# Expert weights in halves: every 2 MB load of an MoE stage split into two 1 MB transfers with semaphores of their own

## What is computed

```python
def hier_moe(n, w_rg, w_re, w_gate, w_up, w_down):
    ...
    hg = jnp.einsum("nd,edf->nef", t, w_gate)
    hu = jnp.einsum("nd,edf->nef", t, w_up)
    act = jax.nn.silu(hg) * hu * gates[..., None].astype(t.dtype)
    return jnp.einsum("nef,efd->nd", act, w_down).reshape(bt, s, d)
```

## Time and profile before

| | |
|---|---|
| median of three runs | 1160.43 us |
| the profiled execution's own time | 1159.52 us |
| its span, first to last instruction | 1157.7 us |
| mean granted TensorE clock | 0.981 of full speed |
| PE busy | 1059.5 us (92%), 7153 matmul instructions |
| DVE, ACT, POOL busy | 550.9, 200.3, 42.4 us |
| DMA | 384.53 MB in 38612 packets, mean 332 GB/s |
| gate and up loads | 64 transfers of 2048 KB, median 27.8 us from issue to landing |
| down loads | 32 transfers of 2048 KB, median 26.1 us from issue to landing |

### The profile page before, as it was taken

The page is one execution under the profiler, slowest core; times in us unless marked ns, Lnnn a source line. Parts: engine busy times, 40 slices in busy tenths (PEclk is TensorE's granted clock), DMA queues, the critical chain, the costliest instruction groups (busy, mean ns, idle before and its releaser), DMA issues.

```text
span 1157.7 us, 17262 instructions
## 1 busy us (share of the span) xinstructions
PE 1059.5 (92%) x7153; PEld 588.5 (51%) x7153; DVE 550.9 (48%) x1078; ACT 200.3 (17%) x457; POOL 42.4 (4%) x38
## 2 busy tenths in 40 slices
PE   8998999998999999999999998899998969797885
PEld 3576776666666656677777542333332323232221
DVE  3583565356535466474434116545443434343333
ACT  1111012131213231311011021111211111111020
POOL 0030110001020000010000000000000000000000
PEclk9899999999999999999999999999999999999898
DMA  9989337988999989743776538999999999999994
GB/s 326 360 233 354 119 133 304 354 336 318 373 380 395 396 331 374 301 166 109 280 286 232 204 132 357 428 412 429 427 425 430 425 428 431 427 427 428 427 428 163
DMA packets 38612, 384.53 MB, mean 332 GB/s; under 512 B 4863, under 2 KB 7551, under 8 KB 10207
## 3 DMA queue, kind: packets, MB, share of 16 engines
q1 hardware_dynamic: 35968, 375.83, 81.1%
q0 software_dynamic: 1568, 5.62, 1.8%
q10 hardware_dynamic: 1008, 2.10, 0.5%
HBM read 375.63 MB, written 7.90 MB: 331 GB/s over the span
## 4 chain that ended last, share of the span: by engine, by line
PE 70%; DMA 16%; DVE 8%; issue 2%; ACT 2%; POOL 1%; ACTq 0%; DVEq 0%; SPq 0%; POOLq 0%
PE ps L605 22%; DMA arena<-w_gu 10%; PE ps L597 7%; PE ps L1025 6%; PE ps L1002 5%; PE ps L1056 5%; DMA arena<-w_proj 4%; PE ps L1040 4%; PE ps L799 4%; PE ps L766 3%; PE ps L587 3%; DMA arena<-w_dn 2%; DVE cst L1775 1%; PE ps L1061 1%; DVE cst L1714 1%
## 5 line engine op out<-in xcount | busy, mean ns | idle before, releaser
L605 PE MATMUL ps<-arena 128*128 128x256 f32 x1456 | 337.2, 386 | 7.9 <-DMA arena<-w_proj 4.5
L605 PEld LDWEIGHTS ps<-arena 128*128 128x128 f32 x1456 | 273.5, 192 | 60.3 <-issue 13.9
L1025 PE MATMUL ps<-arena,cst 128*32 128x512 f32 x1024 | 122.2, 613 | 29.7 <-DMA arena<-w_gu 28.0
L1775 DVE STREAM_TRANSPOSE cst<-ps 128x512 f32<-128x512 f32 x31 | 22.2, 717 | 172.5 <-PE ps L1002 172.5
L597 PE MATMUL ps<-arena 128*64 128x256 f32 x832 | 101.3, 385 | 0.0
L1002 PE MATMUL ps<-arena,cst 128*32 128x512 f32 (+1 forms) x768 | 95.6, 612 | 0.0
L1040 PE MATMUL ps<-arena,stat 128*32 128x512 f32 x512 | 68.0, 652 | 24.6 <-DVE stat L1779 23.2
L1025 PEld LDWEIGHTS ps<-arena,cst 128*32 128x32 f32 x1024 | 32.4, 112 | 113.7 <-issue 82.6
L597 PEld LDWEIGHTS ps<-arena 128*64 128x64 f32 x832 | 55.1, 136 | 37.8 <-issue 14.1
L1797 DVE COPY arena<-ps 32x512 f32<-32x512 f32 x64 | 44.2, 691 | 48.0 <-PE ps L1040 46.6
L1056 PE MATMUL ps<-arena,cst 128*128 128x512 f32 x128 | 57.0, 598 | 9.6 <-ACT cst L1267 9.6
(11 more groups left out here) (261 smaller groups left out, 980.9 us busy)
## 6 DMA issues: line engine op xcount, KB each, us to landing
arena<-w_gu SPq DMA_DIRECT2D x64, 2048.0 KB, 27.8
arena<-w_dn SPq DMA_DIRECT2D x32, 2048.0 KB, 26.1
arena<-w_proj SPq DMA_DIRECT2D x43, 1024.0 KB, 8.1
arena<-kc SPq DMA_DIRECT2D x16, 2048.0 KB, 9.8
arena<-vc SPq DMA_DIRECT2D x16, 2048.0 KB, 8.9
arena<-w_o SPq DMA_DIRECT2D x16, 1024.0 KB, 4.9
arena<-kc SPq DMA_DIRECT2D x8, 1024.0 KB, 8.8
arena<-vc SPq DMA_DIRECT2D x8, 1024.0 KB, 10.1
```

The costliest lines, as they stand in the source:

```text
L605: last = mm(psum[:, regions(v)[j - 1]], left[a], right[:, a], start=first and opens and a == 0, stop=final and a == 1, skip_group_check=True)
L1025: last = mm(ps[g:g + 32, 0, :], xgT[:, s % 2, kt, :], w[:, k, :], start=kt < 4, stop=kt >= KT - 4)
```

## The change

Each piece is loaded as two transfers of 1 MB, and everything that hangs on a piece hangs on its half. A gate and up piece is cut after four of its eight blocks, a down piece after the first of its two blocks; each partition then gets 8 KB per transfer. Every slot has two load semaphores. PE waits for a half before the first matmul that reads it and counts it as used behind the last one; `piece_used` counts halves, six for an expert. SP waits for each half's area by itself. The matmuls, their order and their operands stay as they were, and the waits of ACT and DVE are renumbered.

```diff
-        ring_loaded = [sem(f"ring_loaded{k}") for k in range(RING)]
+        ring_loaded = [[sem(f"ring_loaded{j}_{k}") for k in range(2)] for j in range(RING)]
...
+            def half_piece(u, e, k):
+
+                loaded = (once_loaded[u] if u in once else ring_loaded[slot(u)])[k]
+                if u % 3 < 2:
+                    h = KT // 2 * (u % 3) + 4 * k
+                    sp.dma_start(gate_up(u)[:, 4 * k:4 * k + 4], w_gu[e, :, h:h + 4]).then_inc(loaded, 16)
+                else:
+                    sp.dma_start(down(u)[:, k], w_dn[e, :, k]).then_inc(loaded, 16)
+
             def piece(u, e):
...
+                for k in range(2):
+                    half_piece(u, e, k)
...
             for u in range(10, 3 * BODY + 10):
-                sp.wait_ge(piece_used, u - 9 if u < 16 else u - 7)
-                piece(u, u // 3)
+                for k in range(2):
+                    sp.wait_ge(piece_used, 2 * (u - 10 if u < 16 else u - 8) + k + 1)
+                    half_piece(u, u // 3, k)
...
-                    sp.wait_ge(piece_used, i * (3 * BODY) + (j + 3))
...
+                    for k in range(2):
+                        sp.wait_ge(piece_used, i * (6 * BODY) + (2 * j + k + 5))
...
-                        loaded(i, first, 3 * s + h)
                         w = gate_up(3 * s + h if first else 3 * s + h + 3 * BODY)
                         for k in range(KT // 2):
                             kt = KT // 2 * h + k
                             g = 32 * (kt % 4)
+                            if k % 4 == 0:
+                                loaded(i, first, 3 * s + h, k // 4)
                             last = mm(ps[g:g + 32, 0, :], xgT[:, s % 2, kt, :], w[:, k, :],
                                       start=kt < 4, stop=kt >= KT - 4)
-                        last.then_inc(piece_used, 1)
+                            if k % 4 == 3:
+                                last.then_inc(piece_used, 1)
...
-                    loaded(i, first, 3 * s + 2)
                     w = down(3 * s + 2 if first else 3 * s + 2 + 3 * BODY)
                     pe.wait_ge(ye_copied, i * (4 * BODY) + 4 * (s + 1))
                     for j in range(2):
+                        loaded(i, first, 3 * s + 2, j)
                         for g in range(4):
                             last = mm(ps[32 * g:32 * g + 32, 3, :], actT[:, j, :], w[:, j, 512 * g:512 * g + 512],
                                       start=j == 0, stop=j == 1)
-                    last.then_inc(piece_used, 1)
+                        last.then_inc(piece_used, 1)
```

More of the change, by code:

```diff
@@ L225, in hybrid_step @@
         once = {6: A_N2, 7: A_N2 + PIECE}
-        once_loaded = {u: sem(f"once_loaded{u}") for u in once}
+        once_loaded = {u: [sem(f"once_loaded{u}_{k}") for k in range(2)] for u in once}
         def slot(u):
@@ L519, in _ @@
             sp.dma_start(mst, mst_d).then_inc(mst_loaded, 16)
-            def piece(u, e):
[L522 to L527, removed]
+            def half_piece(u, e, k):
[5 more added lines that the diff above has]
+                    sp.dma_start(down(u)[:, k], w_dn[e, :, k]).then_inc(loaded, 16)
+            def piece(u, e):
+                for k in range(2):
+                    half_piece(u, e, k)
             for o in range(1, 13):
@@ L555, in pieces @@
                         e = sp.value_load(eblk_i[0:1, ds(i * BODY + u // 3, 1)], min_val=0, max_val=NEXP - 1)
-                    sp.wait_ge(piece_used, i * (3 * BODY) + (j + 3))
[L557 to L561, removed]
+                    for k in range(2):
+                        sp.wait_ge(piece_used, i * (6 * BODY) + (2 * j + k + 5))
+                        if u % 3 < 2:
+                            h = KT // 2 * (u % 3) + 4 * k
+                            sp.dma_start(area(A_R[slot(u)], KT // 2, 2 * FF)[:, 4 * k:4 * k + 4], w_gu[ds(e, 1), :, h:h + 4]).then_inc(ring_loaded[slot(u)][k], 16)
+                        else:
+                            sp.dma_start(down(u)[:, k], w_dn[ds(e, 1), :, k]).then_inc(ring_loaded[slot(u)][k], 16)
             sp.wait_ge(blocks_ready, 1)
@@ L1004, in gather, with loaded @@
                 last.then_inc(xg_mm, 1)
-            def loaded(i, first, u):
+            def loaded(i, first, u, k):
                 if first and u in once:
-                    pe.wait_ge(once_loaded[u], 16)
+                    pe.wait_ge(once_loaded[u][k], 16)
                 elif first and u < 6:
-                    pe.wait_ge(ring_loaded[u], 16)
+                    pe.wait_ge(ring_loaded[u][k], 16)
                 else:
-                    pe.wait_ge(ring_loaded[(u - 2) % RING], i * 48 + 16 * ((u - 2) // RING + 1))
+                    pe.wait_ge(ring_loaded[(u - 2) % RING][k], i * 48 + 16 * ((u - 2) // RING + 1))
             def experts(i, first, final):
@@ L1255, in experts @@
                     b = s % BATCH
-                    act.wait_ge(piece_used, i * (3 * BODY) + (3 * s + 2))
+                    act.wait_ge(piece_used, i * (6 * BODY) + (6 * s + 4))
                     copy(part, ps[:, 0, :]).then_inc(gu_copied, 1)
@@ L1259, in experts @@
                     nc.scalar.activation(sg, ps[:, 2, 0:64], ACT.Silu).then_inc(silu_done, 1)
-                    act.wait_ge(piece_used, i * (3 * BODY) + (3 * s + 3))
+                    act.wait_ge(piece_used, i * (6 * BODY) + (6 * s + 6))
                     if first and s == 0:
@@ L1794, in experts @@
                         scale_rows(0, P).then_inc(p_made, 1)
-                    dve.wait_ge(piece_used, i * (3 * BODY) + (3 * s + 3))
+                    dve.wait_ge(piece_used, i * (6 * BODY) + (6 * s + 6))
                     for g in range(2, 4):
```

## The result

The changed kernel takes 1166.72 us (median of 22 runs, 1161.63 to 1168.21), the kernel before in the same series 1164.05 us (22 runs, 1158.29 to 1169.84). The ratio is **1.0027, with a 95% interval of 1.0014 to 1.0040**: 0.27% or about 3 us slower. Against the kernel beside it the forecast was 1.7 us slower (0.15%), at the low edge of that interval; the measured change lies inside the 0.3% called "no change". The forecast in microseconds missed: 1166.72 is 4.6 us above the 1162.1 forecast and just above the range's end of 1166.5. Of these 4.6 us, 3.6 are the level, for the kernel before was itself that much slower over 22 runs than over the three that the forecast was hung on, and the rest is the change.

What follows compares the result with a forecast made beforehand. The DMA engines were taken to bound the experts' stage; start -0.9, rate +4.6 and tail -2.0 us on 1159.5 gave 1161.2, or 1162.1 us on the median, range 1156.9 to 1166.5.

Steps and rivals of the forecast that it cites:

- the 0.3% called "no change": Whole kernel: about 3.5 us is what a measurement can tell from no change; chance of a result within it 0.58.
- The bound: Experts' stage, about 700 us to the end: lasts as long as DMA engines need for pieces 10 to 95, about 421 us.
- The rate, +4.6 us: DMA engines, 86 pieces: nine more packets per engine and piece at 6 ns cost 4.6 us, ends 0 and +8.9.
- the rival that the prediction gave 0.20: Every DMA engine, all 86 pieces: packet price 8 to 11.5 ns, sum +3.3 to +6.0 us; chance 0.20.
- The two prices that the 6 ns were put between: Packet prices from the two longest saturated stretches with mostly 8 KB rows, taken as nearest in size.
- The 2.0 us per transfer: DMA stream: rival that each transfer pays fixed time the queue does not hide, 172 us by this fit; chance 0.03.
- The halves did land apart: Tail: answers the rival that halves land together, leaving today's tail shape and 1164.1 us; chance 0.05.
- The start, -0.9 us: Piece 10: its area is released two matmul groups, 0.86 us, earlier and the stream stays whole; ends 0 and -0.9.
- The tail, -2.0 us: Last expert's pieces 94 and 95: matmuls start on halves, gaining 2.55 or 1.6 us depending on the clock.
- one of the prediction's own signs of being wrong: Tail: a last down piece that still runs in one go was listed among what would show the prediction wrong.
- the 2.55 that the prediction had for this case: Tail: gain of 2.55 us if the last down matmuls run at the full clock, PE done at 1137.6.
- The sum: Whole kernel: 1159.5 - 0.9 + 4.6 - 2.0 = 1161.2 us; on the median 1.7 above 1160.43, 1162.1 us.

Runs made afterwards that it cites:

- e4: Kernel before with halves only at piece 10 and the last expert's three pieces, other pieces whole; ratio to before 1.0009 (0.9990 to 1.0027).
- e5: Kernel before, whole pieces, with unused matmuls in the last expert ahead of its waits to keep PE busy; ratio to before 0.9988 (0.9971 to 1.0005).
- e6: Kernel before with halves at piece 10 and the last expert's pieces, plus unused matmuls in the last expert; ratio to before 0.9987 (0.9972 to 1.0002).
- e8: As e6, with piece 20 also loaded in halves, its first released by piece 12's first half; ratio to before 0.9969 (0.9953 to 0.9985).
- e9: Kernel before, unchanged, profiled again for spread; 427.29 us from first expert matmul to last gate and up matmuls, then 9.98 us to ACT's copy.
- e1: Kernel before with each piece issued as two 1 MB transfers, without the finer waits and releases; ratio to before 1.0040 (1.0016 to 1.0063).
- e2: Kernel before with weights laid out so each single transfer has two 8 KB rows per partition; ratio to before 1.0052 (1.0030 to 1.0075).
- e7: Changed kernel with unused matmuls in the last expert ahead of its waits; ratio to the kernel before 1.0010 (0.9989 to 1.0030).
- e10: Changed kernel, unaltered, profiled again for spread; 429.37 us from first expert matmul to last gate and up matmuls, then 9.01 us to ACT's copy.
- e3: Kernel before with weights laid out so each single transfer has four 4 KB rows per partition; ratio to before 1.0143 (1.0105 to 1.0180).

## Why the prediction was right and where it was wrong

*The bound* was read right. In every run the stage lasts as long as the DMA engines take, but for the gap at piece 20, at a rate that depends on the rows alone: 428, 421 or 409 GB/s.

*The rate, +4.6 us:* right in kind and about in size. Taking for each profile the time from the first load's issue to the last gate and up matmuls, less the idle time at piece 20, the six profiles with 16 KB rows (before, e4, e5, e6, e8, e9) give 422.5 to 424.2, mean 423.6 us, and the five with 8 KB rows (changed, e1, e2, e7, e10) 428.2 to 428.7, mean 428.5: **5.0 us**. The whole times of e1 and e2, 4.7 and 6.0 us slower, lie on either side. But the price per packet was mis-sized: read from the rate it was 8.5 ns instead of 6, above the 7.2 of the longest stretch in the earlier trace rows, and so inside the rival that the prediction gave 0.20, a price of 8 to 11.5 ns. The two prices that the 6 ns were put between were hardly two readings, since the stretch 30:40 lies within 22:40. By the price the term would have been 6.6 us; why only 5.0 arrive at the end of the stage no run shows, and that the term came out near the forecast is in part luck. That a transfer pays no fixed time that shows follows from e1 against e2 (the same 421 GB/s with two transfers and with one). The 2.0 us per transfer that the prediction cited there from the Trainium skill (DMA: Bandwidth & Descriptors, section Anatomy of one DMA — SWDGE (gpsimd) path) are a fit for transfers issued by GpSimd, and the loads here are SP's. The halves did land apart (e7).

*The start, -0.9 us:* the first load came 0.87 us sooner and in the changed kernel the DMA engines have next to no gap behind it (0.2 us at piece 20). But the prediction followed the queue to piece 16 and stopped there; the gap is at piece 20, behind the first combination. In e4, where piece 20 is loaded whole, the 0.9 us do not reach the end of the stage. The changed kernel has no such gap because it halves piece 20 as well and because its stream is slower; e2, with whole pieces at 421 GB/s, shows none there either (share 0.99 and 1.04).

*The tail, -2.0 us:* **this step failed.** The prediction let the second half's matmuls begin by 1136.8 and allowed the low clock only under the down matmuls. In both profiles of the changed kernel the clock had fallen before that, with the last gate and up half, and the matmuls, the turn and the down matmuls all ran at the lower level: 9.01 us, against 8.64 and 9.98 before. So the down piece still ran in one go, one of the prediction's own signs of being wrong. Of 2.0 us, 0.3 are left between the means, and that is within the spread: without the added matmuls the stretch takes 7.84 to 9.98 us in the five profiles that wait for whole pieces (before, e9, e1, e2, e3) and 8.54 to 9.01 in the three with halves. With the clock kept up (e7) the same halves give 6.06 us, 2.58 less than the first profile before, and the 2.55 that the prediction had for this case was right. Of it the clock alone is worth 1.61 (e5, whole pieces, 7.03 us) and the halves 0.97.

*The sum,* from the means of two profiles each: 429.7 against 426.1 to the last gate and up matmuls, +3.6 (forecast +3.7), -0.3 at the tail (forecast -2.0), together +3.3 us; the measured 0.27% is 3.1. That +3.6 falls so near to +3.7 is luck as well: the two profiles of the kernel before differ by 2.4 us in this stretch.

*The level:* the range was set around the median of three runs. The kernel before varies by some 11 us over its 22 runs, and the profiles show three places where an execution gains or loses 1 to 5 us: the clock in the first 50 us of the experts, the clock at the tail, and the clock in the mixer, long before the change can act. The first expert matmul starts between 704.75 us (e1) and 710.05 us (e5) in the twelve profiles. Of the 7.2 us between the spans of the first two profiles, 1.6 lie before it; there, first before and then after the change, PE does in the same time fewer matmuls, at a clock of 0.89 instead of 1.00:

```profile
428.00:444.00 16.00, 13.99 (x147) 9.35 (x149) 8.28 (x16) 4.64 (x15) 2.29 (x1) 1.00 0.78 300
```

```profile
428.00:444.00 16.00, 13.99 (x122) 9.32 (x122) 8.24 (x16) 4.59 (x15) 2.29 (x1) 0.89 0.68 256
```

Runs with whole loads at that point (e2, e5) have the same 0.89 there, so it is not the halves' doing. A single profile and three runs could not show this, and a range in microseconds should have been wider for it.

## What to carry to other kernels

Where loads stand in a deep queue, as here, splitting a transfer costs hardly anything for itself; what it costs comes from the rows that it shortens (5 us of some 423 here): count rows per engine, and split along what keeps each partition's contiguous row long. Finer waits paid here only where the queue is empty, at the start, at the end and at a gap between, so split there alone, and follow a gain at the start through every later release until the queue can no longer run dry. And work cut into small bits between waits can cost the matmul clock just where the last bit is on the path; a few unused matmuls in the waits gave back 3 us there in the profiles.

## What was unexpected

SP's issues got long. The prediction counted 0.33 us for each. Issues of gate and up loads in the loop, by source line (minimum, median and largest in ns), before and after:

```profile
L559 SPq DMA_DIRECT2D arena<-w_gu x41: 332/333/356, 818.7 to 1106.3; - x41
```

```profile
L565 SPq DMA_DIRECT2D arena<-w_gu x82: 333/1928/6002, 819.6 to 1111.3; - x82
```

With twice the packets queued, SP stands in the issue itself, and loads land at most 30.1 us behind it where it was 37.9. It cost nothing here, for the DMA share stays at 1.01 (e1, e2 and e3 have long issues too, with medians of 1.9, 3.8 and 4.2 us), but whatever else stood on SP would have waited.

That a slow TensorE clock makes the DMA engines idle some 40 us later (e9) was not expected either: a bound in one engine does not mean that the others' speed is without effect as long as a queue can run dry.
